# Norm squares in fp32 pairs, and sample matmuls with loads of their own, in an eight-core hybrid decoder step

## What is computed

```python
def _rmsnorm(x, g):
    xf = x.astype(jnp.float32)
    y = xf * lax.rsqrt(jnp.mean(xf * xf, axis=-1, keepdims=True) + RMS_EPS)
    return (y * g.astype(jnp.float32)).astype(x.dtype)

def _layer(...):
    h = _rmsnorm(x, norm1_g)
    z = h @ w_in
    ...
    ys, hr, hi = _s5(zu, h0_re, h0_im, ...)
    gy = jax.nn.gelu(ys, approximate=False)
    ys = gy * jax.nn.sigmoid(gy @ w_glu + b_glu)
    ...
    x = x + m @ w_out
    h2 = _rmsnorm(x, norm2_g)
    gate, up = jnp.split(h2 @ w_gate_up, [D_FF], axis=-1)
    x = x + (jax.nn.silu(gate) * up) @ w_down
```

## Time and profile before

| what | value |
|---|---|
| median of three runs | 3657.71 us (3657.15 to 3664.83) |
| profiled execution, its own time | 3657.15 us |
| its span on the slowest core (core 0) | 3655.6 us |
| spans of all cores | 3640.0 to 3655.6 us |
| mean granted TensorE clock, by core | 0.985 to 0.988 |
| PE busy | 3500.2 us, 96% |
| DVE busy | 1617.7 us, 44% |
| ACT busy | 1136.3 us, 31% |
| POOL busy | 610.6 us, 17% |

### The profile page before, as it was taken

The page is one execution under the profiler, slowest core; times in us unless marked ns, Lnnn a source line. Parts: engine busy times, 40 slices in busy tenths (PEclk is TensorE's granted clock), DMA queues, the critical chain, the costliest instruction groups (busy, mean ns, idle before and its releaser), DMA issues.

```text
span 3655.6 us, 65790 instructions; the slowest of 8 cores (3640.0 to 3655.6 us)
## 1 busy us (share of the span) xinstructions
PE 3500.2 (96%) x23912; PEld 1976.1 (54%) x22376; DVE 1617.7 (44%) x2889; ACT 1136.3 (31%) x2146; POOL 610.6 (17%) x799
## 2 busy tenths in 40 slices
PE   6799999999999999999999899999999999999998
PEld 3566666666666666666664344444444444444443
DVE  8845455465554555533244331354214442254323
ACT  4443134432344323423134220243103421042202
POOL 4233210322103321030000200002000110002000
PEclk9899999999999999999999999999999999999999
DMA  7534457435574345854448544584446644474443
GB/s 162 121 72 72 112 148 152 76 70 114 144 158 74 70 114 144 178 104 80 71 74 193 112 77 74 94 173 75 75 74 116 149 70 79 74 143 79 80 71 87
DMA packets 252798, 384.04 MB, mean 105 GB/s; under 512 B 157632, under 2 KB 180800, under 8 KB 246848
## 3 DMA queue, kind: packets, MB, share of 16 engines
q0 software_dynamic: 67968, 243.30, 39.8%
q1 hardware_dynamic: 184512, 136.53, 12.9%
HBM read 567.06 MB, written 56.12 MB: 170 GB/s over the span
## 4 chain that ended last, share of the span: by engine, by line
PE 87%; DVE 4%; issue 3%; DMA 3%; ACT 1%; SPq 1%; DVEq 0%; ACTq 0%; POOL 0%; POOLq 0%
PE ps L675 83%; DMA yT<-X 1%; PE ps L708 1%; DVE SC L562 1%; DVE H L732 1%; PE ps L1039 1%; PE ps L666 1%; PE ps L1113 1%; DVE X L1255 0%; DMA scv<-CIN 0%; PE ps L914 0%; PE ps L1081 0%; SPq L633 0%; DMA dy<-YY 0%; DMA X<-xsT 0%
## 5 line engine op out<-in xcount | busy, mean ns | idle before, releaser
L675 PE MATMUL ps<-H,RING 128*128 128x512 bf16 (+2 forms) x12160 | 2192.8, 340 | 23.7 <-DVE H L732 9.7
L675 PEld LDWEIGHTS ps<-H,RING 128*128 128x128 bf16 x12160 | 1190.0, 98 | 965.4 <-issue 52.4
L675 PE MATMUL ps<-R,RING 128*128 128x384 bf16 (+2 forms) x6400 | 1162.8, 339 | 26.3 <-DMA R<-dy 16.4
L675 PEld LDWEIGHTS ps<-R,RING 128*128 128x128 bf16 x6400 | 624.2, 98 | 525.4 <-issue 43.5
L657 POOL DMA_DIRECT2D RING<-wpk x472 | 254.1, 539 | 2627.2 <-PE ps L675 2419.2
L1277 DVE TENSOR_TENSOR R<-SC,ps 128x384 bf16<-128x384 f32 (+2 forms) x440 | 255.8, 583 | 787.3 <-PE ps L675 774.1
L1276 ACT ACTIVATE SC<-ps 128x384 f32<-128x384 f32 (+2 forms) x440 | 226.1, 515 | 1208.1 <-PE ps L675 1204.4
L1255 DVE TENSOR_TENSOR X<-X,ps 128x384 f32<-128x384 f32 (+2 forms) x480 | 269.8, 582 | 449.1 <-PE ps L675 443.9
L706 ACT ACTIVATE H<-X 128x384 bf16<-128x384 f32 (+2 forms) x304 | 156.5, 539 | 198.0 <-DVE X L1255 178.4
L732 DVE SCALAR_TENSOR_TENSOR H<-X,PRM,SC 128x384 bf16<-128x384 f32 (+2 forms) x304 | 183.0, 672 | 35.5 <-ACT SC L713 35.4
L1249 POOL TENSOR_TENSOR R<-TB,SC 128x384 bf16<-128x384 f32 (+1 forms) x160 | 168.2, 1065 | 110.7 <-DVE SC L1246 99.0
(11 more groups left out here) (177 smaller groups left out, 1662.5 us busy)
## 6 DMA issues: line engine op xcount, KB each, us to landing
RING<-wpk POOLq DMA_DIRECT2D x440, 512.0 KB, 6.9
TAB<-stash SPq DMA_DIRECT2D x21, 1792.0 KB, 9.0
stash<-TAB SPq DMA_DIRECT2D x15, 1792.0 KB, 6.9
R<-stash SPq DMA_DIRECT2D x7, 1792.0 KB, 14.0
RING<-wpk POOLq DMA_DIRECT2D x32, 384.0 KB, 6.4
du<-R SPq DMA_DIRECT2D x32, 256.0 KB, 8.8
UU<-du SPq DMA_DIRECT2D x32, 256.0 KB, 7.5
dy<-YY SPq DMA_DIRECT2D x32, 256.0 KB, 7.0
```

The lines of the kernel that those rows point to most:

```text
L675: subs.append((lambda e, u=u, kw=kw, c=c, src=src, i=i: e.matmul(ps[:, 0:blk.n], lhsT=u.ap(kw, c), rhs=src(blk), start=(i == 0), stop=(i = ...
```

## The change

Three edits.

1. In `norm`, outside the final norm, the norm of layer 0 at the start of half 0, and the one at the change of halves, the eight tiles are taken in four pairs. ACT squares both tiles of a pair into fp32 scratch (from `SP_` in half 0, from `SQ` in half 1, both slots claimed first), DVE adds the two into `H` in bf16, and one matmul against the ones follows. That makes four matmuls in place of eight, and four DVE additions that were not there.
2. In `ssm_f` the matmuls of the samples follow those of the prompt as groups of their own, instead of standing between them.
3. `keep` is gone: every matmul is issued with its own weight load. In V the order within a group of eight changes too, so that the two row halves alternate.

```diff
-    def keep(e, out, lhsT, rhs, start, stop, tile=(128, 128), pos=(0, 0), skip=False):
-        return e.add_instruction(mybir.InstMatmult(
-            start_tensor_calc=start, stop_tensor_calc=stop, tile_size=tile, tile_position=pos, ldweights=False, bass_skip_group_check=skip,
...
     def norm(half, blk, l, which, src=None):
...
+        pairs = which != "fg" and src is None and not (half == 0 and l == 0 and which == "n1")
...
-        for kt in range(8):
+        QP = SQ if half == 1 else SP_
+        for k2 in range(4 if pairs else 0):
+            ta, tb2 = QP.new(), QP.new()
+            for t, kt in ((ta, 2 * k2), (tb2, 2 * k2 + 1)):
+                act(lambda e, kt=kt, t=t: e.activation(out=t[:, 0:n], in_=xin(kt)[0], func=AF.Square), xin(kt)[1], [(t,)], n)
+            tt(lambda k2=k2: hq(k2), lambda ta=ta: ta[:, 0:n], lambda tb2=tb2: tb2[:, 0:n], ALU.add, [(ta,), (tb2,)], qkeys(k2, blk), n)
+            S.pe([(lambda e, k2=k2: e.matmul(ps[:, 0:n], lhsT=ONESB[:], rhs=hq(k2), start=(k2 == 0), stop=(k2 == 3)),
+                   qkeys(k2, blk) + [C_("ONESB")], MMN(n))], [(ps,)], FULL)
+        for kt in range(0 if pairs else 8):
...
-                            if hs and h == 0:
-                                subs.append((lambda e, q=q, g2=g2, ri=ri: keep(
-                                    e, gsb[64 * g2:64 * g2 + 64, ri * 64 + q * 16:ri * 64 + q * 16 + 16], Wv(0)[:, q, g2, ri, :],
-                                    us()[:, q, g2, :], q == 0 and ri == 0, True, (128, 64), (0, 64 * g2), True), tkk + [(ut_, 1)], MMN(16)))
-            S.pe(subs, [(gg,)] + ([(gsb,)] if hs else []), (128, 64))
+            S.pe(subs, [(gg,)], (128, 64))
+            if hs:
+                subs = []
...
+                            subs.append((lambda e, q=q, g2=g2, ri=ri: e.matmul(
+                                gsb[64 * g2:64 * g2 + 64, ri * 64 + q * 16:ri * 64 + q * 16 + 16], lhsT=Wv(0)[:, q, g2, ri, :],
+                                rhs=us()[:, q, g2, :], start=(q == 0 and ri == 0), stop=True, tile_position=(0, 64 * g2),
+                                skip_group_check=True), tkk + [(ut_, 1)], MMN(16)))
+                S.pe(subs, [(gsb,)], (128, 64))
...
-            S.pe(subs, [(yb[0],), (yb[1],)] + ([(ysb,)] if hs else []), FULL)
+            S.pe(subs, [(yb[0],), (yb[1],)], FULL)
+            if hs:
+                ysb = PP.new()
...
+                S.pe(subs, [(ysb,)], FULL)
...
-                    for ri, oo in ((0, (0, 768)), (1, (256, 512))):
+                    for i, (o, ri, kk) in enumerate(((0, 0, 0), (256, 1, 0), (512, 1, 1), (768, 0, 1))):
                         for g2 in range(2):
...
-                            subs.append((lambda e, q=q, g2=g2, h=h, o=oo[1], ri=ri, rows=rows: keep(
-                                e, yo(g2, h, q), CDv(h)[rows, q, ri, :], vq(o, q, g2), False, ri == 1, (64, 128), (64 * g2, 0), True),
-                                tkk + [(vt, 0), (vt, 1)], MMN(64) * 0.5))
+                            subs.append((lambda e, q=q, g2=g2, h=h, o=o, ri=ri, i=i: e.matmul(
+                                yo(g2, h, q), lhsT=CDv(h)[64 * g2:64 * g2 + 64, q, ri, :], rhs=vq(o, q, g2),
+                                start=False, stop=(i == 3), tile_position=(64 * g2, 0), skip_group_check=True), tkk + [(vt, 0), (vt, 1)], MMN(64) * 0.6))
```

More of the change, by code:

```diff
@@ L1042, in ssm_f @@
                                 tkk + [(ut_, 0)], MMN(64)))
-                            if hs and h == 0:
-                                subs.append((lambda e, q=q, g2=g2, ri=ri: keep(
-                                    e, gsb[64 * g2:64 * g2 + 64, ri * 64 + q * 16:ri * 64 + q * 16 + 16], Wv(0)[:, q, g2, ri, :],
-                                    us()[:, q, g2, :], q == 0 and ri == 0, True, (128, 64), (0, 64 * g2), True), tkk + [(ut_, 1)], MMN(16)))
-            S.pe(subs, [(gg,)] + ([(gsb,)] if hs else []), (128, 64))
+            S.pe(subs, [(gg,)], (128, 64))
+            if hs:
+                subs = []
+                for q in range(4):
+                    for g2 in range(2):
+                        for ri in range(2):
+                            subs.append((lambda e, q=q, g2=g2, ri=ri: e.matmul(
[3 more added lines that the diff above has]
+                S.pe(subs, [(gsb,)], (128, 64))
             w2 = lambda ap: ap.rearrange("p (r x) -> p r x", r=2)
@@ L1075, in ssm_f @@
             yb = [PP.new(), PP.new()]
-            ysb = PP.new() if hs else None
             yo = lambda g2, h, q: yb[g2][:, h * 256 + q * 64:h * 256 + q * 64 + 64]
@@ L1091, in ssm_f @@
                         start=False, stop=False, skip_group_check=True), tkk + [(ut_, 0)], MMN(64)))
+            S.pe(subs, [(yb[0],), (yb[1],)], FULL)
             if hs:
+                ysb = PP.new()
+                subs = []
                 for q in range(4):
-                    for ri in range(2):
-                        for g2 in range(2):
-                            gl = 2 * q + g2
-                            ysl = lambda gl=gl: ysb[:, gl * 16:gl * 16 + 16]
-                            zsl = lambda q=q, ri=ri, g2=g2: AS0Z[:, g2, ri, 4 * f + q, :]
-                            if g2 == 0:
-                                fn = lambda e, q=q, ri=ri, ysl=ysl, zsl=zsl: e.matmul(ysl(), lhsT=CDv(0)[:, q, ri, :], rhs=zsl(), start=False, stop=(ri == 1),
-                                                                                   skip_group_check=True)
-                            else:
-                                fn = lambda e, q=q, ri=ri, ysl=ysl, zsl=zsl: keep(e, ysl(), CDv(0)[:, q, ri, :], zsl(), False, ri == 1, skip=True)
-                            subs.append((fn, tkk + [C_("AS0Z")], MMN(16)))
-            S.pe(subs, [(yb[0],), (yb[1],)] + ([(ysb,)] if hs else []), FULL)
+                    for g2 in range(2):
+                        gl = 2 * q + g2
+                        subs.append((lambda e, q=q, g2=g2, gl=gl: e.matmul(
+                            ysb[:, gl * 16:gl * 16 + 16], lhsT=KTv(0)[:, q, g2, :], rhs=us()[:, q, g2, :], start=(gl == 0), stop=False,
+                            skip_group_check=True), tkk + [(ut_, 1)], MMN(16)))
+                        for ri in range(2):
+                            subs.append((lambda e, q=q, g2=g2, gl=gl, ri=ri: e.matmul(
+                                ysb[:, gl * 16:gl * 16 + 16], lhsT=CDv(0)[:, q, ri, :], rhs=AS0Z[:, g2, ri, 4 * f + q, :], start=False, stop=(ri == 1),
+                                skip_group_check=True), tkk + [C_("AS0Z")], MMN(16)))
+                S.pe(subs, [(ysb,)], FULL)
             vq = lambda o, q, g2: vt[64 * g2:64 * g2 + 64, o + q * 64:o + q * 64 + 64]
```

10 lines of the change are left out of this document (removed).

## The result

The changed kernel takes 3628.72 us, median of four runs (3627.59 to 3631.75), beside 3657.71 us for the kernel before in the same session; the ratio is 0.9916, with a 95% interval from 0.9897 to 0.9936. The forecast was 3622 us within 3602 to 3650. Against the execution from which the sum was made (3657.15 us) the profiled one, 3627.59 us, is 29.6 us shorter where the sum had 35.9.

What follows compares the result with a forecast made beforehand. PE, busy 96% of the span, was taken as the bound; -24.4 + 4 - 4.5 - 10 - 6 + 3 + 2 = -35.9 us from 3657.15 gave 3621.2, with the median's 0.56 3622 us; range 3602 to 3650.

Steps and rivals of the forecast that it cites:

- Norm matmuls: Paired norms of both halves: 140 of 320 matmuls go from PE's stream, 180 stay, -24.4 us.
- Additions: 140 new DVE additions in the norms, mostly hidden behind the other block: +4 us, from 0 to +15.
- Place A: Third block in half 0, layers 0 to 2: more products cover PE's wait on `H`, -4.5 us, from -8 to 0.
- some 10 us: Sign at the norms: PE's waits on the new additions or on `H` should stay under this in all.
- second rival: At the norms, sums come too late on DVE: 3687 us without the other places' gains, 3667 with; chance 0.09, half slower.
- Place B: State-space part in half 1: V behind 24 products loses three waits and their slow clock, -10 us, from -12 to -4.
- the clock there stays at 1.0: Sign in half 1's state-space part: V starts without a wait after 24 products and the clock must stay at 1.0.
- Start: Up to layer 0's fourth V, 11.0 us of PE work moves into idle time: -6 us, from -11 to +6.
- Own loads: State-space part, each matmul loading its own weights: V +3 us over 32 groups, samples +2 us over 16 groups.
- 0 to 26 us of the bounds: Range for V's own loads: less than 0 excluded, +26 us at the 27 ns pace of the `prep` product.
- third rival: In V and the samples, 1536 more loads are not hidden, 99 ns each, 152 us: 3769 us; chance 0.03.
- Rival 1: Rearrangement brings nothing: waits at places A to C are replaced by others of the same length, 3642 us; chance 0.10.

Runs made afterwards that it cites:

- experiment 8: Kernel before with the paired norm squares in half 1 alone: 3627.4 us against 3648.0 us for the kernel before, by spans.
- experiment 5: Changed kernel with each of the 140 pair additions made twice on DVE, PE waiting for the second: 3683.9 us, 63 us more than the changed kernel.
- experiment 6: Kernel before with pairs alone, GpSimd's first next-table products in half 0's layers 0 to 2 waiting for the third block's last multiplication: 3600.4 against 3648.0 us.
- experiment 1: Kernel before with the paired norm squares alone, state-space part as before: 3611.3 us against 3646.6 us for the kernel before, by spans.
- experiment 2: Changed kernel with norm squares as before, keeping samples apart and own weight loads: 3650.9 us against 3646.6 us for the kernel before.
- experiment 4: Kernel before with all 1536 kept weights loaded again, every order unchanged: 3659.8 us against 3646.6 us for the kernel before.
- experiment 3: Changed kernel with V's pairs sharing one weight load again, 1024 loads fewer: 3608.9 us, 12 us less than the changed kernel.
- experiment 9: Changed kernel with 64 small matmuls and their 64 loads put at the head of PE's list: 3611.2 us, 10 us less than the changed kernel.
- experiment 7: Changed kernel with the u read and y write moved in 2 KB pieces instead of 128 B: 3621.6 us against the changed kernel's 3620.9 us.

## Why the prediction held, step by step

- **Norm matmuls, -24.4 us.** Right: 180 matmuls, columns as counted. In half 1 alone the pairs give 12.1 us of columns and 9 of waits [experiment 8].
- **Additions, +4 us.** Right in size: 2.5 us of waits. That the margins are thin was right too, and experiment 5 gives their measure: three quarters of a second addition are paid.
- **Place A, -4.5 us (-8 to 0).** Wrong, in sign: the waits on `H` went up by 4 us on core 0 to 13.7, past the "some 10 us" that the prediction had set as the sign of its second rival, though not on the additions (2.5 us), and with one more stretch at a low clock. The step counted 2.6 us more cover against one addition, and that part held (2.41 to 0.45 us for the first wait); it took the pace of the eight multiplications as fixed. They went from 5.19 to 7.87 us, because in the new order five of them, not two, stand beside GpSimd's products [experiment 6].
- **Place B, -10 us.** The waits went as said, with 24 products ahead of V; wrong is where that order comes from. I read it off the new order of the whole change and put it down to the state-space part; that part alone keeps the waits, the pairs alone remove them [experiments 1, 2, 8]. In the changed kernel stalls at packet borders then take 7.3 us back in half 1 on core 0 (2.81, 0.94, 3.59), and the sign that the clock there stays at 1.0 was not met: 0.62 and 0.59 behind two of them.
- **Start, -6 us.** Right: about 5 us of idle time less, with the state-space part.
- **Own loads, +3 and +2 us.** Mis-sized: +13 us for the same 1536 loads in an unchanged order [experiment 4], and +12 for V's 1024 in the changed one [experiment 3]. The direct price was right, V lasts 1.11 us as before; the price that I left out is that of fetching. It lay within the 0 to 26 us of the bounds, for another reason. Experiment 9 shows that a shift alone is worth 8 to 10 us, so how much of the 12 and 13 is the number of loads, and how much where the packets' borders came to lie, is not separated. Both show in the number of stops of 0.9 us or more on all eight cores: 23 in the kernel before and 51 with its loads made its own [experiment 4]; 59 in the changed kernel, 42 with V's loads shared [experiment 3], 40 with the list shifted [experiment 9]. The rule of the Trainium skill weighed there ("TensorE: Matmul & The Clock Gate", Part 3) decided nothing: V, whose matmuls alternate between row halves, lost nothing, and by that rule its loads can overlap, so the third rival should not have counted them.
- **Rivals.** That the sums come too late did not happen, though it was one addition away. Rival 1, waits replaced by others, came true in part: at place A, and in half 1 through the stops at packet borders.
- **What I did not foresee:** the change of halves, from the last V of layer 3 to the last V of layer 0 in half 1, took 12 to 15 us less on cores 0 and 1 with the same order there. The change did not bring it. In the kernel before the same stretch took 467.3 us on core 6 of the very execution in which cores 0 to 2 took 480.3 to 485.9, and in experiment 4, with the order of before everywhere, cores 0 to 2 took 468.0 to 469.8. What cores 0 to 2 had there and core 6 had not are waits of PE on ACT, the longest on core 0 this one:

```profile
1968.19 13.26 PE L675 MATMUL ps<-H,RING 128*128 128x512 bf16 x48 [5.72 <-ACT TB L1167]
```

  Why they come on some cores and not on others stays open.

The sum was right to 6 or 7 us by luck: place A and the loads came out 10 and 8 us worse than forecast, and the execution from which the sum was made had, on its slowest cores, some 12 us of waits and low clock at the change of halves that the changed kernel's did not have. By the median over the cores the change is worth 26 us, 10 less than the sum.

## What to carry to other kernels

Where short matmuls with own loads stand close together, count instructions as well as columns: V, G and Y, 112 matmuls and as many loads, pass here in 2.8 us (2394.09 to 2396.88), and when the next packet is not there, PE stops for 1 to 4 us on core 0; sharing loads, or a shift of the whole list, moves that. Before DVE work is put on a thin margin, look at what GpSimd does in the same microseconds. Before a sum is made against one execution, compare its cores: a wait that only some of them have is no part of what a change can win. And when an order is made by a scheduler, try each part of a change alone before giving it the credit for a wait.

## What the runs showed of the hardware

- PE's instructions arrive in packets of 16.4 KB, 256 instructions. The packet of the stop at 3238.8 starts 1.2 us into it, in the DMA queues between 3238 and 3240 us, and lands at 3240.9; PE goes on 1.4 us later:

```profile
q8 instruction: 1, 0.02, 3.0%
```

  In streams of 512 columns 128 matmuls last 27.6 us, and no stop of 0.9 us or more stands further than 20 matmuls from the state-space part in these traces; between 589.34 and 597.55 us 123 matmuls passed in 8.2 us, the stop included. Stops of 3.59 us appeared in three kernels, in one of them [experiment 7] with most of the small transfers gone.
- 128 instructions at the head of PE's list made the kernel 8 to 10 us faster, though they do nothing.
- A DVE multiplication of 272 columns from two SBUF inputs lasts 0.49 us alone and 1.30 to 1.54 us beside GpSimd's products, and then ends 0.30 us after a product does.
